# Latent attention on one core: the rope rows' halves exchanged by VectorE, one product tile less, and ScalarE's queue between two pairs of heads in another order

## The chip, the cores and the metric

The kernel runs on one core of a Trainium2 chip. Five engines work side by side and wait for each other by semaphores: TensorE (PE in the rows) multiplies, VectorE (DVE), ScalarE (ACT) and GpSimd (POOL) work element by element, and SyncE (SP) issues loads. The metric is the device time of one execution in microseconds; less is better. Matrix results land in PSUM, eight banks of 128 partitions by 512 fp32 values;

## The reference

The whole kernel computes a two-layer transformer block and then a second two-layer block, for 512 tokens of width 1024, in fp32. The change touches only the last mixer, a latent attention with 16 heads:

```python
q = jnp.einsum('bsr,rhd->bshd', q_c, w_uq)            # q_c: 512 x 256, w_uq: 256 x 16 x (128 + 64)
q_nope, q_rope = q[..., :128], q[..., 128:]
q_rope = apply_rope(q_rope, cos, sin)                 # x1, x2 = halves of 32
k_rope = apply_rope(k_r, cos, sin)
q_lat = jnp.einsum('bshd,rhd->bshr', q_nope, w_uk)
s = q_lat . kv_c + q_rope . k_rope                    # scaled, masked by chunks of 64, softmax in blocks of 128
o = jnp.einsum('bshr,rhd->bshd', p . kv_c, w_uv)
return (o * jax.nn.silu(z)) @ w_out

def apply_rope(x, cos, sin):
    return concatenate([x1 * cos - x2 * sin, x2 * cos + x1 * sin])
```

## The kernel before

Activations are kept transposed: features on the 128 partitions, the 512 tokens along a row. Each fp32 product is made of three matmuls of rounded parts (`mm3`, lines 964 to 966: high by high, high weight by low data, low weight by high data). For that every weight unit, 128 partitions by 1024 columns (eight tiles of 128), goes through four steps: SP loads it into one of four `raw` slots, ScalarE copies it to its high part (`split_hi`, line 540), GpSimd subtracts to get the low part (`split_lo`, line 447), and TensorE uses it. Semaphores count units: `raw_in` loaded, `hi_done`, `w_ready` both parts there, `unit_used` used by TensorE. Unit u needs unit u - 4 used, since the slots are a ring of four.

The order of all work is written out by hand, engine by engine. The latent attention goes over eight pairs of heads. Each pair r takes four units from `u0 = O_H + 2 + 4 r`: two of gate columns z (u0, u0 + 1), one of query weights for the NEXT pair (u0 + 2), and one with the value tiles of this pair and the latent query tiles of the next (u0 + 3). On TensorE a pair runs so (`pair_of_heads`): the first z product; score blocks 0 and 1; four of the eight k-tiles of the second z product; then steps m = 2 to 10, which interleave transposes of the probabilities (`o_transpose`, line 1434), scores (`o_scores`, lines 1423 to 1426) and the product with the latent (`o_latent`, line 1442). Two k-tiles of the second z product stand at m = 5 and two at m = 9. Behind them come `queries` for the next pair, `values` and `latent_queries`. There are eight score blocks m: blocks 0 to 3 are the four query blocks of the first head with 128, 256, 384 and 512 keys, blocks 4 to 7 those of the second.

`queries` makes four tiles: the 128 nope rows of each head into two gate banks, the rope rows of both heads (64 + 64 partitions) into bank 2, and the same rope rows with their halves of 32 exchanged into bank 3. The exchange is in the weights: `pack_weights` lays out tiles `rope` and `swap`.

VectorE's softmax has two steps per block, maximum (`o_max_of`, lines 2083 and 2085) and product with the reciprocal of the sum (`o_norm`, lines 2090 and 2094); ScalarE has the exponential (line 890) between them. At a pair's end VectorE subtracts for the second latent (line 2099), for the two nope tiles (`nope_lo`, line 2067), turns the rope rows (`rotate`, lines 2073 to 2078) and multiplies the two gate products (line 2122). ScalarE at that point applies Silu to z (line 920), makes high parts (lines 902, 869), splits units, copies the latent queries (`keep_latent`, lines 881 and 883), makes the high parts of the rope rows in both partition halves (`rope_hi`, line 876) and scales one eighth of the residual (line 932). GpSimd makes the rope rows' low parts (`rope_lo`, line 507) and multiplies the residual (line 516).

ScalarE's functions come in table sets; a table load (ACT_TABLE_LOAD) is put in by the compiler, once ahead of the first Silu and once ahead of the first Exp of a pair. A loop round holds two pairs, r = 0 and r = 1 (`Fori(0, PAIRS - 2, 2)`), so pairs 0, 2 and 4 stand at the start of a round, and pairs 6 and 7 behind the loop.

Of the kernel before, what the change touches and what calls it, by code (L numbers as in the profile page):

```python
# [37 lines left out]
RING = 4  # L38
# [67 lines left out]
PI = 3.1415925  # L106


def build(nc, xT, weights, cols, rows, c_row, rel, onehot, w2, posc, ada, ws, bs, pcnt, pos, out):

    ctx = ExitStack()
    with ctx:
# [309 lines left out]
        def _(pool):  # L422
# [22 lines left out]
            def split_lo(slot, unit):  # L445
                pool.wait_ge(hi_done, unit + 1)
                pool.tensor_tensor(wsp[:, slot, 1, :], raw[:, slot, :], wsp[:, slot, 0, :].bitcast(F32),  # L447
                                   ALU.subtract).then_inc(w_ready, 1)
# [61 lines left out]
            for u in range(O_C + RING, O_H + 5):  # L510
                split_lo(u % RING, u)
# [6 lines left out]
            with pool.Fori(0, PAIRS - 1) as hp:  # L518
                for k in range(RING):
                    u = O_H + 5 + k  # L520
                    split_lo(u % RING, hp * RING + u)
# [5 lines left out]
            for u in range(O_H + 5 + RING * (PAIRS - 1), UNITS):  # L527
                split_lo(u % RING, u)
# [3 lines left out]
        def _(act):  # L532
            def split_hi(u, i=0):
# [6 lines left out]
                act.activation(wsp[:, u % RING, 0, :], raw[:, u % RING, :], ACT.Copy).then_inc(hi_done, 1)  # L540
# [325 lines left out]
            def nope_hi(r, hp):  # L866
                for e in range(2):
                    act.wait_ge(uq_mm, hp * 3 + (3 * r + e + 1))
                    act.activation(qns[:, e, 0, :], bank[GATE_BANKS[r % 2][e]][:, :], ACT.Copy).then_inc(n_hi, 1)

            def rope_hi(r, hp):

                for e in range(2):
                    act.wait_ge(r_part, hp * 4 + (4 * r + e + 3))
                    for half in range(2):
                        act.activation(qrs[e][0][half * HD:half * HD + HD, :], r_raw[e], ACT.Copy).then_inc(r_hi, 1)
# [27 lines left out]
            def pair_of_heads(r, hp, last):  # L904

                u0 = O_H + 2 + RING * r
                split_hi(u0 + 3, hp)
# [16 lines left out]
                else:  # L924
# [3 lines left out]
                    rope_hi(r + 1, hp)  # L928
                    split_hi(u0 + 6, hp)
                j = hp + r  # L930
                act.wait_ge(mod_x, j + (16 + DC + 1))
                act.activation(hT[:, j, :], hT[:, j, :], ACT.Identity, scale=modg[:, 1, bass.ds(j + 16, 1)],
                               bias=modg[:, 1, bass.ds(j + 24, 1)]).then_inc(alpha_done, 1)

# [9 lines left out]
            rope_hi(0, 0)  # L944
# [16 lines left out]
        def _(pe):  # L961
# [420 lines left out]
            def queries(r, hp, u):  # L1382
# [3 lines left out]
                for n in range(4):  # L1386
                    if first and n == 2:
                        pe.wait_ge(c_normed, 3)
                    if first and n == 3:
                        pe.wait_ge(kr_ready, 1)  # L1390
# [3 lines left out]
                    x.then_inc(uq_mm if n < 3 else unit_used, 1)  # L1394
# [51 lines left out]
            def pair_of_heads(r, hp, last):  # L1446
# [7 lines left out]
                project(u0 + 1, z[1][:, :], hp, part=range(4))  # L1454
                for m in range(2, 11):
                    if m in (5, 9):
                        project(u0 + 1, z[1][:, :], hp, part=range(m // 4 * 2 + 2, m // 4 * 2 + 4))
# [33 lines left out]
        def _(dve):  # L1491
# [780 lines left out]
```

## Times and profile before

| | us |
|---|---|
| three runs | 2046.43, 2047.74, 2047.75 |
| median | 2047.74 |
| the profiled execution | 2044.9 |
| its span | 2043.0 |
| mean granted TensorE clock | 0.988 |
| TensorE busy in the span | 1943.9 (95%) |
| VectorE / ScalarE / GpSimd busy | 972.6 / 836.8 / 815.2 |

The loop over pairs runs from about 1653 to 1924 us of the span. In a row of the timeline the columns are start us, duration us, engine, line, operation, out<-in, shapes, count, and in brackets how long the engine was idle before and what it waited for. A matmul's end is modelled and overlaps the next one's start: TensorE's progress is read from the starts. "x2" or "x4" joins neighbours of one kind, and then the duration is that of all of them.

### The profile page before, as it was taken

How to read it: one execution, taken by the hardware profiler on the slowest of the kernel's cores; microseconds unless marked ns; L12 is line 12 of the kernel's file. 1: busy time of each engine (PE TensorE's matmuls, PEld its weight loads, DVE VectorE, ACT ScalarE, POOL GpSimd, SP SyncE). 2: the span in 40 equal slices, each digit the busy share in tenths (PEclk: the TensorE clock that was granted, in tenths of full speed). 3: DMA queues.
4: the chain of work that ended last, by engine and by line, in shares of the span. 5: the costliest groups of instructions: out<-in, count | busy, mean ns of one | idle time of the engine just before them, and what ended most of it. 6: DMA issues, size and time to landing. Idle time of an engine off the chain costs nothing.

```text
span 2043.0 us, 29277 instructions
## 1 busy us (share of the span) xinstructions
PE 1943.9 (95%) x9688; PEld 1623.0 (79%) x9688; DVE 972.6 (48%) x2289; ACT 836.8 (41%) x1520; POOL 815.2 (40%) x390
## 2 busy tenths in 40 slices
PE   7999999999989999999999998999999799999896
PEld 5897888888777989878888887877888587777784
DVE  5554655321445777456652115557411644545414
ACT  4564222232443777442222224222223356666523
POOL 3633544444374011135454442545444145252440
PEclk9999999999999999999999998999999999999998
DMA  7532554322242122135442222322223122121221
GB/s 242 166 100 95 192 176 169 105 94 92 73 165 75 38 70 78 39 107 194 164 166 100 94 96 77 106 93 98 92 94 102 42 73 73 51 72 52 73 72 41
DMA packets 70027, 209.56 MB, mean 103 GB/s; under 512 B 9739, under 2 KB 15115, under 8 KB 69948
## 3 DMA queue, kind: packets, MB, share of 16 engines
q1 hardware_dynamic: 57724, 174.72, 26.0%
q10 hardware_dynamic: 12224, 33.85, 5.1%
q8 instruction: 42, 0.69, 0.1%
q14 instruction: 37, 0.30, 0.0%
HBM read 196.90 MB, written 8.49 MB: 101 GB/s over the span
## 4 chain that ended last, share of the span: by engine, by line
PE 62%; issue 21%; POOL 9%; DVE 6%; ACT 2%; POOLq 0%; DVEq 0%; ACTq 0%
PE bank L964 16%; PE bank L966 16%; PE bank L965 16%; POOL wsp L447 9%; PE bank L1266 3%; PE bank L1235 1%; PE bank L1246 1%; PE bank L1423 1%; PE bank L1130 1%; PE bank L1442 1%; PE bank L1107 1%; PE bank L1018 1%; PE bank L1434 1%; PE bank L1118 1%; DVE gen L2094 1%
## 5 line engine op out<-in xcount | busy, mean ns | idle before, releaser
L447 POOL TENSOR_TENSOR wsp<-raw,wsp 128x1024 fp32r<-128x1024 f32 x294 | 730.7, 2491 | 1001.9 <-ACT wsp L540 1001.7
L964 PE MATMUL bank<-xs,wsp 128*128 128x512 f32 x1320 | 522.5, 396 | 19.2 <-issue 8.4
L965 PE MATMUL bank<-xs,wsp 128*128 128x512 f32 x1320 | 516.7, 391 | 0.0
L966 PE MATMUL bank<-xs,wsp 128*128 128x512 f32 x1320 | 516.6, 391 | 0.0
L540 ACT ACTIVATE wsp<-raw 128x1024 fp32r<-128x1024 f32 x294 | 307.5, 1052 | 235.3 <-PE bank L966 206.7
L964 PEld LDWEIGHTS bank<-xs,wsp 128*128 128x128 f32 x1320 | 249.6, 189 | 76.1 <-issue 15.1
L964 PE MATMUL bank<-xk,wsp 128*128 128x512 f32 x752 | 293.6, 390 | 9.8 <-DVE xk L1548 5.1
L965 PE MATMUL bank<-xk,wsp 128*128 128x512 f32 x752 | 293.0, 390 | 0.0
L966 PE MATMUL bank<-xk,wsp 128*128 128x512 f32 x752 | 292.9, 390 | 0.0
L966 PEld LDWEIGHTS bank<-xs,wsp 128*128 128x128 f32 x1320 | 249.4, 189 | 52.5
L965 PEld LDWEIGHTS bank<-xs,wsp 128*128 128x128 f32 x1320 | 249.8, 189 | 51.2 <-issue 1.0
L1548 DVE TENSOR_TENSOR xk<-mid,xk 128x512 fp32r<-128x512 f32 x86 | 61.1, 710 | 379.1 <-ACT xk L583 379.1
L583 ACT ACTIVATE xk<-mid 128x512 fp32r (+1 forms) x86 | 54.3, 632 | 324.1 <-PE bank L966 324.1
L964 PEld LDWEIGHTS bank<-xk,wsp 128*128 128x128 f32 x752 | 141.2, 188 | 41.0 <-DVE xk L1548 6.3
L966 PEld LDWEIGHTS bank<-xk,wsp 128*128 128x128 f32 x752 | 141.2, 188 | 29.2
L965 PEld LDWEIGHTS bank<-xk,wsp 128*128 128x128 f32 x752 | 141.3, 188 | 29.1
L1598 DVE CUSTOM_DVE_ANT_0 gen<-gen 128x1024 f32<-128x1024 f32 x48 | 125.8, 2620 | 13.0 <-issue 13.0
L599 ACT ACTIVATE tmp<-tmp 128x512 f32<-128x512 f32 x44 | 27.8, 632 | 245.2 <-DVE tmp L1586 245.2
L1588 DVE TENSOR_TENSOR mid<-bank,rstd 128x512 f32 (+1 forms) x44 | 30.4, 692 | 155.6 <-PE bank L966 155.6
L746 ACT ACTIVATE mid<-mid,stat 128x128 f32<-128x128 f32 (+3 forms) x128 | 70.8, 555 | 35.7 <-DVE stat L1850 35.5
L1266 PE MATMUL bank<-mid 128*128 128x64 f32 x640 | 82.4, 276 | 0.0
L1266 PEld LDWEIGHTS bank<-mid 128*128 128x128 f32 x640 | 77.1, 193 | 0.0
(297 smaller groups left out, 2438.5 us busy)
## 6 DMA issues: line engine op xcount, KB each, us to landing
raw<-weights SPq DMA_DIRECT2D x294, 512.0 KB, 3.5
gen<-ada ACTq DMA_DIRECT2D x48, 512.0 KB, 3.6
tmp<-mid SPq DMA_DIRECT2D x64, 128.0 KB, 3.0
bias_b<-bias_row ACTq DMA_DIRECT2D x1, 4096.0 KB, 37.3
mid<-bias_b SPq DMA_DIRECT2D x8, 512.0 KB, 3.9
hT<-xT SPq DMA_DIRECT2D x2, 1024.0 KB, 9.6
bias_a<-bias_row ACTq DMA_DIRECT2D x1, 2048.0 KB, 17.5
mid<-bias_a SPq DMA_DIRECT2D x8, 256.0 KB, 2.9
```

Of the source, the lines that this page charges most:

```text
L447: pool.tensor_tensor(wsp[:, slot, 1, :], raw[:, slot, :], wsp[:, slot, 0, :].bitcast(F32), ALU.subtract).then_inc(w_ready, 1)
L540: act.activation(wsp[:, u % RING, 0, :], raw[:, u % RING, :], ACT.Copy).then_inc(hi_done, 1)
L583: act.activation(xk[:, k % 2, 0, :], mid[:, i * RING + k, :], ACT.Copy).then_inc(xk_hi, 1)
L599: act.activation(tmp[:, 2 + p, :], tmp[:, p, :], ACT.Silu).then_inc(silu_ready, 1)
L746: act.activation(b_s[b][:, r, 0:w], b_s[b][:, r, 0:w], ACT.Exp, scale=-1.0, bias=stat[:, b, r:r + 1], accum_out=stat[:, b, 4 + r:5 + r]).t ...
L964: pe.matmul(dst, w[0], x[0], start=first, stop=False)
L965: pe.matmul(dst, w[0], x[1], start=False, stop=False)
L966: return pe.matmul(dst, w[1], x[0], start=False, stop=last)
L1266: x = pe.matmul(dst[:, (1 + r) * HD:(2 + r) * HD], b_pt[b][:, r, kb * P:kb * P + P], vtok[:, r, kb * P + pp * HD:kb * P + pp * HD + HD], s ...
L1548: dve.tensor_tensor(xk[:, k % 2, 1, :], mid[:, i * RING + k, :], xk[:, k % 2, 0, :].bitcast(F32), ALU.subtract).then_inc(xk_ready, 1)
L1588: dve.tensor_tensor(mid[:, i * 2 + p, :], bank[2 * p + 1][:, :], rstd[:, :], ALU.mult).then_inc(up_free, 1)
L1598: dve.tensor_tensor_reduce(out=ada_st[k], in0=ada_st[k], in1=cond, scale=1.0, scalar=0.0, op0=ALU.mult, op1=ALU.add, accum_out=mod_sum[:, ...
```

## The change

- `queries` makes three tiles. Bank 3 is no longer written by TensorE there, and `uq_mm` counts two per pair.
- `rotate` goes head by head, with four instructions: 64 rows of bank 2 by cos; two products of 32 rows each by sin, from bank 2 into the other half's rows of bank 3; and the difference. The first head's rotation stands where `rotate` stood, the second's behind the two gate products. `r_part` counts six per pair.
- ScalarE: `rope_hi` is called per head. The split of u0 + 3, which opened a pair, is now at the end of the pair before, between the two heads; behind the residual stands an Exp of one column, then the second head's copies.
- TensorE: 3 + 2 + 3 k-tiles of the second z product, where there were 4 + 2 + 2.
- The splits of the query unit take 768 columns and those of the value unit 512 (`columns_of`); the loads stay at 1024. The weights' layout is as it was.

```diff
+def columns_of(u):
+    return (768, 512, UNIT, UNIT)[(u - O_H) % 4] if O_H <= u < O_O else UNIT
...
             for u in range(O_C + RING, O_H + 5):
-                split_lo(u % RING, u)
+                split_lo(u % RING, u, columns_of(u))
...
-            def rope_hi(r, hp):
-
-                for e in range(2):
-                    act.wait_ge(r_part, hp * 4 + (4 * r + e + 3))
-                    for half in range(2):
-                        act.activation(qrs[e][0][half * HD:half * HD + HD, :], r_raw[e], ACT.Copy).then_inc(r_hi, 1)
+            def rope_hi(e, r, hp):
+
+                act.wait_ge(r_part, hp * 6 + (6 * r + 3 * e + 3))
+                for half in range(2):
+                    act.activation(qrs[e][0][half * HD:half * HD + HD, :], r_raw[e], ACT.Copy).then_inc(r_hi, 1)
...
                 u0 = O_H + 2 + RING * r
-                split_hi(u0 + 3, hp)
                 for m in range(10):
...
                     keep_latent(r + 1, hp)
-                    rope_hi(r + 1, hp)
+                    rope_hi(0, r + 1, hp)
                     split_hi(u0 + 6, hp)
+                    split_hi(u0 + 7, hp)
...
                                bias=modg[:, 1, bass.ds(j + 24, 1)]).then_inc(alpha_done, 1)
+                if not last:
+                    act.activation(credit[:, 10:11], eps[:, 0:1], ACT.Exp)
+                    rope_hi(1, r + 1, hp)
...
-            rope_hi(0, 0)
+            rope_hi(0, 0, 0)
+            rope_hi(1, 0, 0)
+            split_hi(O_H + 5)
...
-                for n in range(4):
+                for n in range(3):
                     if first and n == 2:
                         pe.wait_ge(c_normed, 3)
-                    if first and n == 3:
-                        pe.wait_ge(kr_ready, 1)
...
-                    x.then_inc(uq_mm if n < 3 else unit_used, 1)
+                    x.then_inc(uq_mm if n < 2 else unit_used, 1)
...
-                project(u0 + 1, z[1][:, :], hp, part=range(4))
+                project(u0 + 1, z[1][:, :], hp, part=range(3))
                 for m in range(2, 11):
                     if m in (5, 9):
-                        project(u0 + 1, z[1][:, :], hp, part=range(m // 4 * 2 + 2, m // 4 * 2 + 4))
+                        project(u0 + 1, z[1][:, :], hp, part=range(3, 5) if m == 5 else range(5, DC))
...
-            def rotate(r, hp):
-
-                dve.wait_ge(unit_used, hp * RING + (O_H + 1 + RING * r))
-                dve.tensor_tensor(tmp[:, 0, :], bank[2][:, :], cosb, ALU.mult).then_inc(r_part, 1)
-                dve.tensor_tensor(bank[3][:, :], bank[3][:, :], sinb, ALU.mult).then_inc(r_part, 1)
-                dve.wait_ge(r_part, hp * 4 + (4 * r + 2))
-                for e in range(2):
-                    half = slice(e * HD, e * HD + HD)
-                    dve.tensor_tensor(r_raw[e], tmp[half, 0, :], bank[3][half, :], ALU.add).then_inc(r_part, 1)
+            def rotate(e, r, hp):
+
+                head = slice(e * HD, e * HD + HD)
+                if e == 0:
+                    dve.wait_ge(unit_used, hp * RING + (O_H + 1 + RING * r))
+                dve.tensor_tensor(tmp[head, 0, :], bank[2][head, :], cosb[head, :], ALU.mult).then_inc(r_part, 1)
+                for src, dst in ((0, 32), (32, 0)):
+                    at = slice(e * HD + src, e * HD + src + 32)
+                    x = dve.tensor_tensor(bank[3][e * HD + dst:e * HD + dst + 32, :], bank[2][at, :], sinb[at, :], ALU.mult)
+                x.then_inc(r_part, 1)
+                dve.wait_ge(r_part, hp * 6 + (6 * r + 3 * e + 2))
+                dve.tensor_tensor(r_raw[e], tmp[head, 0, :], bank[3][head, :], ALU.subtract).then_inc(r_part, 1)
...
-                    rotate(r + 1, hp)
+                    rotate(0, r + 1, hp)
...
+                if not last:
+                    rotate(1, r + 1, hp)
```

Three places in the order of instructions. The first is ScalarE between pair 6 and pair 7, from the first split behind `nope_hi` on. Before (L540 is a split, L881 and L883 `keep_latent`, L876 `rope_hi`, L932 the residual, L890 the exponential):

```order
L540 ACTIVATE wsp<-raw 128x1024 [waits unit_used,raw_in0]
L881 ACTIVATE gen<-bank4 128x512 [waits lat_mm]
L883 ACTIVATE gen<-bank5 128x512 [waits unit_used]
L876 ACTIVATE mid_r<-tmp 64x512 [waits r_part]
L876 ACTIVATE mid_r<-tmp 64x512
L876 ACTIVATE mid_r<-tmp 64x512 [waits r_part]
L876 ACTIVATE mid_r<-tmp 64x512
L540 ACTIVATE wsp<-raw 128x1024 [waits unit_used,raw_in1]
L932 ACTIVATE hT<-hT,modg 128x512 [waits mod_x]
L540 ACTIVATE wsp<-raw 128x1024 [waits unit_used,raw_in2]
L890 ACT_TABLE_LOAD
L890 ACTIVATE bank0,stat<-bank0,stat 128x128 [waits o_nm]
```

In the changed kernel (L546, L886, L888, L881, L937 and L895 are the same things, L940 the new Exp):

```order
L886 ACTIVATE gen<-bank4 128x512 [waits lat_mm]
L888 ACTIVATE gen<-bank5 128x512 [waits unit_used]
L881 ACTIVATE mid_r<-tmp 64x512 [waits r_part]
L881 ACTIVATE mid_r<-tmp 64x512
L546 ACTIVATE wsp<-raw 128x768 [waits unit_used,raw_in1]
L546 ACTIVATE wsp<-raw 128x1024 [waits unit_used,raw_in2]
L937 ACTIVATE hT<-hT,modg 128x512 [waits mod_x]
L940 ACT_TABLE_LOAD
L940 ACTIVATE credit<-eps 128x1
L881 ACTIVATE mid_r<-tmp 64x512 [waits r_part]
L881 ACTIVATE mid_r<-tmp 64x512
L895 ACTIVATE bank0,stat<-bank0,stat 128x128 [waits o_nm]
```

The split that stood between the residual and the first exponential is now ahead of the residual, and the table load and the new Exp stand ahead of the second head's two copies. (This split has 1024 columns only here, in front of pair 7; elsewhere it has 512.)

The second place is ScalarE at the start of a loop round. Before:

```order
L945 ISA
L539 ISA [waits raw_in2]
L540 ACT_TABLE_LOAD
L540 ACTIVATE wsp<-raw 128x1024 [waits unit_used]
L889 ISA
L890 ACTIVATE bank6,stat<-bank6,stat 128x128 [waits o_nm]
```

In the changed kernel, the end of a round, and behind the dots its start:

```order
L937 ACTIVATE hT<-hT,modg 128x512
L940 ACT_TABLE_LOAD
L940 ACTIVATE credit<-eps 128x1
L879 REGISTER_ALU
L881 ACTIVATE mid_r<-tmp 64x512 [waits r_part]
L881 ACTIVATE mid_r<-tmp 64x512
L955 REGISTER_ALU
L955 COMPARE_AND_BRANCH
...
L955 ISA
L895 ACT_TABLE_LOAD
L895 ACTIVATE bank6,stat<-bank6,stat 128x128 [waits o_nm]
```

A table load stands at a round's start in both. The one ahead of the new Exp, at the round's end, comes to it.

The third is VectorE at the end of a pair, here pair 6. Before (L2067 is `nope_lo`, L2073 to L2078 `rotate`, L2122 the gate products, L2083 the next pair's first maximum):

```order
L2067 TENSOR_TENSOR gsp<-bank6,gsp 128x512 [waits n_hi]
L2067 TENSOR_TENSOR gsp<-bank7,gsp 128x512 [waits n_hi]
L2073 TENSOR_TENSOR tmp<-bank2,gen 128x512 [waits unit_used]
L2074 TENSOR_TENSOR bank3<-bank3,gen 128x512
L2078 TENSOR_TENSOR tmp<-tmp,bank3 64x512 [waits r_part]
L2078 TENSOR_TENSOR tmp<-tmp,bank3 64x512
L2122 TENSOR_TENSOR mid<-bank0,mid 128x512 [waits z_ready,uv_mm]
L2122 TENSOR_TENSOR mid<-bank1,mid 128x512 [waits z_ready,uv_mm]
L2083 TENSOR_REDUCE stat<-bank0 128x1 [waits o_qk]
```

In the changed kernel (L2075, L2083 to L2089, L2133 and L2094):

```order
L2075 TENSOR_TENSOR gsp<-bank6,gsp 128x512 [waits n_hi]
L2075 TENSOR_TENSOR gsp<-bank7,gsp 128x512 [waits n_hi]
L2083 TENSOR_TENSOR tmp<-bank2,gen 64x512 [waits unit_used]
L2086 TENSOR_TENSOR bank3<-bank2,gen 32x512 x2
L2089 TENSOR_TENSOR tmp<-tmp,bank3 64x512 [waits r_part]
L2133 TENSOR_TENSOR mid<-bank0,mid 128x512 [waits z_ready,uv_mm]
L2133 TENSOR_TENSOR mid<-bank1,mid 128x512 [waits z_ready,uv_mm]
L2083 TENSOR_TENSOR tmp<-bank2,gen 64x512
L2086 TENSOR_TENSOR bank3<-bank2,gen 32x512 x2
L2089 TENSOR_TENSOR tmp<-tmp,bank3 64x512 [waits r_part]
L2094 TENSOR_REDUCE stat<-bank0 128x1 [waits o_qk]
```

The four instructions between `nope_lo` and the gate products (two over all 128 partitions, two over 64) have become four for the first head alone; the same four for the second head stand behind the gate products, ahead of the maximum.

## Rows read from the trace of the kernel before

**Rows 1.** The profile page's first line.
```profile
span 2043.0 us, 29277 instructions
```
**Rows 2.** Table of stages, one pair of heads.
```profile
1728.90:1763.30 34.40, 33.34 (x179) 27.32 (x177) 16.99 (x43) 21.73 (x45) 13.19 (x8) 1.00 0.18 61
```
**Rows 3.** Timeline of TensorE, end of a pair.
```profile
1748.88 0.48 PE L964 MATMUL bank<-gsp,wsp 128*128 128x512 f32 x1
...
1752.83 0.39 PE L966 MATMUL bank<-gsp,wsp 128*128 128x512 f32 x1
...
1754.42 0.39 PE L964 MATMUL bank<-xk,wsp 128*128 128x512 f32 x1
...
1757.14 0.39 PE L964 MATMUL bank<-xs,wsp 128*128 128x512 f32 x1
```
**Rows 4.** Timeline of VectorE, the same stretch.
```profile
1752.53 0.69 DVE L2067 TENSOR_TENSOR gsp<-bank,gsp 128x512 fp32r<-128x512 f32 x1 [0.40 <-ACT gsp L869]
1754.62 0.69 DVE L2073 TENSOR_TENSOR tmp<-bank,gen 128x512 f32<-128x512 f32 x1 [1.40 <-PE bank L966]
...
1763.17 0.29 DVE L2083 TENSOR_REDUCE stat<-bank 128x1 f32<-128x128 f32 x1 [4.50 <-PE bank L1426]
```
**Rows 5.** Timeline of ScalarE, from this pair into the next.
```profile
1757.34 0.60 ACT L883 ACTIVATE gen<-bank 128x512 f32<-128x512 f32 x1
1757.84 2.59 ACT L876 ACTIVATE mid_r<-tmp 64x512 fp32r<-64x512 f32 x4
...
1761.41 0.80 ACT L932 ACTIVATE hT<-hT,modg  x1
1762.12 1.04 ACT L540 ACTIVATE wsp<-raw 128x1024 fp32r<-128x1024 f32 x1
1763.18 1.28 ACT L890 ACT_TABLE_LOAD   x1
1764.47 0.34 ACT L890 ACTIVATE bank<-bank,stat 128x128 f32<-128x128 f32 x1
```
**Rows 6.** Timeline of TensorE, the next pair.
```profile
1762.58 0.38 PE L1423 MATMUL bank<-gen 128*128 128x128 f32 x2
...
1766.45 0.27 PE L1434 MATMUL bank<-ident,gen 128*128 128x128 f32 x1
1766.55 0.81 PE L1423 MATMUL bank<-gen 128*128 128x384 f32 x2
...
1767.55 0.38 PE L1434 MATMUL bank<-ident,gen 128*128 128x128 f32 x2
...
1770.11 0.55 PE L1434 MATMUL bank<-ident,gen 128*128 128x128 f32 x3 [0.63 <-DVE gen L2094]
...
1780.29 0.39 PE L966 MATMUL bank<-xs,wsp 128*128 128x512 f32 x1
1781.04 0.66 PE L1434 MATMUL bank<-ident,gen 128*128 128x128 f32 x4 [0.36 <-DVE gen L2094]
```
**Rows 7.** Timeline of VectorE, the first two products.
```profile
1765.16 0.35 DVE L2094 TENSOR_SCALAR gen<-bank,stat 128x128 f32<-128x128 f32 x1
...
1766.86 0.48 DVE L2094 TENSOR_SCALAR gen<-bank,stat 128x256 f32<-128x256 f32 x1
```
**Rows 8.** Groups by line and shape: the nearest rows for new operations.
```profile
L2058 DVE TENSOR_TENSOR bank<-bank,gen 64x512 f32<-64x512 f32 x1 | 0.7, 700 | 0.0
...
L554 ACT ACTIVATE credit<-eps 128x1 f32<-128x1 f32 x1 | 0.2, 203 | 0.0
```
**Rows 9.** Timeline of GpSimd, rope_lo of two heads.
```profile
1759.18 2.61 POOL L507 TENSOR_TENSOR mid_r<-tmp,mid_r 64x512 fp32r<-64x512 f32 x2 [3.27 <-ACT mid_r L876]
```
**Rows 10.** Timelines of VectorE and TensorE before the first pair.
```profile
1650.39 1.29 DVE L2067 TENSOR_TENSOR gsp<-bank,gsp 128x512 fp32r<-128x512 f32 x2
...
1651.95 0.48 PE L964 MATMUL bank<-gsp,wsp 128*128 128x512 f32 x1
```
**Rows 11.** Waits from 1650 to 1895: total us, times, longest.
```profile
PE bank L1434 <- DVE gen L2094: 7.0, 14, 0.7
```

More of the change, by code:

```diff
@@ L442, in _, with split_lo @@
             pool.memset(credit[:, 8:9], 0.0).then_inc(za_silu, 2)
-            def split_lo(slot, unit):
+            def split_lo(slot, unit, w=UNIT):
                 pool.wait_ge(hi_done, unit + 1)
-                pool.tensor_tensor(wsp[:, slot, 1, :], raw[:, slot, :], wsp[:, slot, 0, :].bitcast(F32),
+                pool.tensor_tensor(wsp[:, slot, 1, 0:w], raw[:, slot, 0:w], wsp[:, slot, 0, 0:w].bitcast(F32),
                                    ALU.subtract).then_inc(w_ready, 1)
@@ L520, in _ @@
                     u = O_H + 5 + k
-                    split_lo(u % RING, hp * RING + u)
+                    split_lo(u % RING, hp * RING + u, columns_of(u))
                     if k == 0:
@@ L527, in _ @@
             for u in range(O_H + 5 + RING * (PAIRS - 1), UNITS):
-                split_lo(u % RING, u)
+                split_lo(u % RING, u, columns_of(u))
         @block.scalar
@@ L539, in split_hi @@
                     act.wait_ge(unit_used, i * RING + (u + 1 - RING))
-                act.activation(wsp[:, u % RING, 0, :], raw[:, u % RING, :], ACT.Copy).then_inc(hi_done, 1)
+                w = columns_of(u + i * RING if isinstance(i, int) else u)
+                act.activation(wsp[:, u % RING, 0, 0:w], raw[:, u % RING, 0:w], ACT.Copy).then_inc(hi_done, 1)
             def scaled_hi(gain, base):
@@ L867, in nope_hi @@
                 for e in range(2):
-                    act.wait_ge(uq_mm, hp * 3 + (3 * r + e + 1))
+                    act.wait_ge(uq_mm, hp * 2 + (2 * r + e + 1))
                     act.activation(qns[:, e, 0, :], bank[GATE_BANKS[r % 2][e]][:, :], ACT.Copy).then_inc(n_hi, 1)
-            def rope_hi(r, hp):
-                for e in range(2):
-                    act.wait_ge(r_part, hp * 4 + (4 * r + e + 3))
-                    for half in range(2):
-                        act.activation(qrs[e][0][half * HD:half * HD + HD, :], r_raw[e], ACT.Copy).then_inc(r_hi, 1)
+            def rope_hi(e, r, hp):
+                act.wait_ge(r_part, hp * 6 + (6 * r + 3 * e + 3))
+                for half in range(2):
+                    act.activation(qrs[e][0][half * HD:half * HD + HD, :], r_raw[e], ACT.Copy).then_inc(r_hi, 1)
             def keep_latent(r, hp):
@@ L2123, in pair_of_heads @@
                                       ).then_inc(mid_ready, 1)
+                if not last:
+                    rotate(1, r + 1, hp)
             nope_lo(0, 0)
-            rotate(0, 0)
+            rotate(0, 0, 0)
+            rotate(1, 0, 0)
             with dve.Fori(0, PAIRS - 2, 2) as hp:
```

## The prediction

> **What bounds the kernel now.** I read the page's span first, then the table of stages. The edit touches only the attention loop, where one pair of heads takes 34.4 us and TensorE is busy for 33.3 us of it at a granted clock of 1.00 (2.4 GHz) [rows 1, 2]. So a matmul that is taken out should shorten the span unless something else is then late. TensorE's own timeline gives the price of a matmul: the rows print about 390 ns each, but they overlap, and what counts is from start to start. From 1748.88 to 1752.83 there are 17 starts in 3.95 us; over whole stretches, 12 matmuls (values and latent queries) lie between 1754.42 and 1757.14: 2.72/12 = 0.227 us each [rows 3].
>
> Next I looked for the gaps inside one pair. There are two, both while TensorE waits for the normalised probabilities: before the three transposes of 1770.11, and before the four of 1781.04 [rows 6]. The table of waits has 14 of this kind over the seven pairs [rows 11]. The second gap runs from the end of the last z matmul's turn (1780.29 + 0.23 = 1780.52) to 1781.04: 0.52 us. Everything else I count from s, the start of a pair's first score matmul, which is 1762.58 here.
>
> **Part 1, no product tile.** `queries` loses two mm3 groups, six matmuls: 6 x 0.227 = 1.36 us. It runs once ahead of the loop and at seven boundaries between pairs. Is it on the path there? What follows it waits for other engines. The values wait for the low half of the second latent and the latent queries for the second `nope_lo`, which starts on VectorE at 1752.53 and lasts 0.69, so ends at 1753.22 [rows 4]. The values will start at 1754.42 - 1.36 = 1753.06 (VectorE's subtraction for them is before that `nope_lo` in its queue) and the latent queries, 6 matmuls later, at 1754.42. Room: 1.2 us. The whole 1.36 counts, and the next pair's scores start at 1762.58 - 1.36 = 1761.22. Seven boundaries: 9.5 us.
>
> At the first `queries` it is different. There `nope_lo` ends at 1650.39 + 1.29 = 1651.68, held by the keys' rotation, which does not move; the latent queries started at 1651.95 [rows 10]. They can come at about 1651.8: 0.2 us gained, the rest becomes a new wait.
>
> **Part 2, the rotation in halves.** Four VectorE instructions become eight. The 64x512 product from PSUM, crossing partitions, lasted 0.70 us [rows 8]; a 32x512 one is not in the trace. Free size and not partitions set these times (128x512 0.69, 64x512 0.70 [rows 4, 8]), so I take 0.70; the bounds are the small VectorE rows at 0.35 [rows 7] and twice the nearest, 1.4. `rotate(0)`: starts when bank 2 is complete, 1.36 us sooner than 1754.62, at 1753.26; four steps of 0.7 end at 1756.1. The two gate products (1.29) follow, to 1757.4, and `rotate(1)` ends at 1760.2. Behind it in VectorE's queue is the first maximum, which can start 0.59 after s, at 1761.81 [rows 4, 7]: 1.6 us of room, so these 2.8 us of extra VectorE work cost nothing. Without that cover each would count in full.
>
> **Part 3, ScalarE's order.** I lay the new queue out with the times of the old one [rows 5]. The second latent copy, at 1757.34, comes at 1755.98; 0.50 later, at 1756.48, the first head's two copies (2.59/4 = 0.65 each), to 1757.8; by then `rotate(0)` is done. A split costs 1.05 for 1024 columns; 0.83 for 768 and 0.6 for 512 scale from that with the 0.63 of the 512-column copy as a check; with the overlap of 0.09 that successive rows show they end at 1759.1. The residual (0.80) ends at 1759.9, the table load 1.28 and the dummy Exp 0.20 [rows 8] at 1761.3, the second head's copies at 1762.6. So the first exponential starts at s + 1.4. It was at 1764.47, s + 1.89, behind a 1024-column split and the load. The load has moved from in front of the exponential to a place where ScalarE had time, and `split_hi(u0 + 7)` with it.
>
> The POOL queue: `rope_lo` for the second head now waits for copies that end at 1762.6 and lasts 1.3 [rows 9], to 1763.9. It is first wanted by the fifth score block, after 1770.11. The splits behind it are 768 and 512 wide and wanted a pair later. For the first head it ends near 1759.1, 2 us ahead of the scores. No cost. SP's loads follow these splits, and are hidden as before.
>
> **Part 4, three z matmuls moved.** Between the first two score blocks and the first transpose stand 9 matmuls and no longer 12, and at the end of the pair 9 and no longer 6. The first transpose is asked for at s + 1.11 + 9 x 0.227 = s + 3.2. Its data came 1.04 after the exponential (1764.47 to 1765.16 + 0.35), now s + 2.4. Scores of block 2 start at s + 3.3 and end at s + 4.3; the second transposes need the second product, which ended at 1766.86 + 0.48 = 1767.34, 2.87 after the first exponential, so s + 4.3 [rows 5 to 7]. That just fits. Then the chain maximum, exponential, product of block 2 is 0.68 earlier and the wait of 1770.11 stays as long as it was. At the end of the pair the three extra matmuls (0.68) fill the 0.52 gap and run 0.16 beyond. Net: 0.52 us in each of eight pairs, 4.2 us.
>
> **Part 5, loop heads.** The order listing shows two loads of the table at the start of a loop round: the dummy's, and one still in front of the first exponential of r = 0. This concerns pairs 2 and 4; pair 0 has only the second, pair 6 stands behind the loop and has only the first. In those two the first exponential starts at s + 1.4 + 1.28 = s + 2.7. The second product ends at s + 5.6, the second transposes wait for it, and block 2's product follows at s + 7.9 and not s + 6.85: 1.05 us each, 2.1 us lost. Pair 7's split between the two rope copies is 1024 wide and not 512: 0.45 us later on ScalarE, 0.4 lost.
>
> Where a page and the rows differ: the load's row lasts 1.28 us, the split in front ends at 1762.12 + 1.04 = 1763.16, the load starts at 1763.18 and the exponential at 1764.47 [rows 5], so nothing else is paid around it. The Trainium skill ("ScalarE: Activation LUTs", section "What ACT_TABLE_LOAD costs") gives the same 1283 ns and adds a drain of about 1380 ns for a switch of sets, 2.66 us in all; by that rule the result is the third case below, and the trace does not agree with it.
>
> **Sum.** 9.5 + 0.2 + 4.2 - 2.1 - 0.4 = 11.4 us. The profiled execution took 2044.9 us (span 2043.0 [rows 1] and 1.9 around it), so 2033.5. The median of the runs shown is 2047.74, 2.8 above it; the same gain gives 2036.3.
>
> **The rivals.**
> Second case, ScalarE late at every boundary: the margin of Part 4 (second product at s + 4.3 against 4.3) is nothing. If ScalarE's new queue is 0.6 us longer than my sum of rows (six hand-overs at 0.1 more each), five boundaries lose 0.6 and two more lose it on top of theirs: 4.2 us. Gain 7.2, time 2040.5. For it: nine instructions in a row on one engine. Against: the old queue's rows follow each other within 0.02 to 0.1 us. The other way, if the second load costs nothing, the gain is 13.5: 2034.2.
> Third case, no measurable difference: a table load holds ScalarE for twice its row, 2.6 us. Then the first exponential comes at s + 2.7 in the five boundaries with one load, which by Part 5 costs 1.05 us each, and another 2.6 later in the two with two loads, where the wait is already on the path: 5.3 + 5.2 = 10.5 us. Gain 1.3, time 2046.4. For it: the load is moved in front of other work of this engine, where no row shows one. Against it: the rows of Part 5, with nothing around the load.
> Fourth case, slower: the 32-row products. `rotate(1)` ends after four of them and holds the maximum and, through the second head's copies, the first exponential. Each extra e on one costs 4e - 1.1 a boundary (1.1 is the room between 1760.2 and the copies' start at 1761.3). To eat the 11.4 us and 4.1 more takes 2.2 us at each of seven, e = 0.83: a 32x512 product of 1.53 us. It decides from there; at 1.7 us (e = 1.0, 2.9 us a boundary) the kernel is at 2056.6. Nothing but the missing row speaks for it; the 64-row one at 0.70 speaks against.
> That the change does less than it says is in Part 5: two of seven loads are doubled, not moved.
>
> **Chances.** Forecast case 0.64, the second with its faster wing 0.24 (0.18 and 0.06), the third 0.08, the fourth 0.04. A difference under 0.2% (4.1 us) is what a measurement here cannot tell from none. Faster than that: the first two, 0.88; within: 0.08; slower: 0.04. The range holds the first two cases: 2032.8 to 2041.5.
>
> **What would show it.** TensorE's starts from the first query matmul to the first z matmul 6.9 us apart, not 8.26; a pair of 32.5 us, and 33.6 where the loop starts a round; no gap before the four last transposes; the 32x512 rows at 0.70; the load before the second head's copies, and the first exponential at s + 1.4. Wrong if the second transposes wait at every pair, or if a new gap stands before the latent queries inside the loop.

## The result, and the profile after

| | before | changed |
|---|---|---|
| median of four runs, us | 2047.09 | 2033.74 |
| lowest and highest | 2045.34, 2047.75 | 2032.06, 2035.49 |
| span of the profiled execution | 2043.0 | 2030.2 |
| ratio, 95% interval | | 0.9936 [0.9922, 0.9949] |

The forecast was 2036.3 (2032.8 to 2041.5). The kernel is 13.4 us faster by the medians and 12.8 by the spans, where the sum said 11.4. (The forecast started from a median before of 2047.74; the fourth run put it at 2047.09, and that is 0.65 of the 2.6 us between 2036.3 and 2033.74.) In the changed kernel line numbers are 5 to 14 higher; L974 to L976 are the three matmuls of `mm3`, L1431 to L1434 the scores, L1442 the transposes, L1450 the product with the latent.

The table of stages, cut at the first score matmul of pairs 1, 3 and 4, answers to [rows 2]. Its first column is the stretch, its second the length; the busy times of PE, PE's weight loads, DVE, ACT and POOL follow, and the granted clock is the third column from the right:

```profile
1691.56:1724.11 32.55, 31.84 (x171) 26.27 (x170) 19.84 (x46) 21.20 (x45) 11.54 (x7) 1.00 0.20 65
1757.71:1790.28 32.57, 31.86 (x171) 26.26 (x170) 19.84 (x46) 21.20 (x45) 11.56 (x7) 1.00 0.20 64
1790.28:1823.88 33.60, 32.30 (x171) 26.18 (x170) 19.75 (x46) 22.52 (x46) 11.52 (x7) 1.00 0.19 62
```

A pair takes 32.55 us where it took 34.5, and 33.6 at the start of a loop round. VectorE is busy 2.8 us more in a pair than before. ScalarE is busy 1.3 us more in the last row than in the two above it: that is the second table load.

TensorE through pair 3, which starts at s = 1757.71, answers to [rows 6] and, in the last two lines, to [rows 3]:

```profile
1757.71 0.38 PE L1431 MATMUL bank<-gen 128*128 128x128 f32 x2
...
1760.89 0.27 PE L1442 MATMUL bank<-ident,gen 128*128 128x128 f32 x1
1761.00 0.81 PE L1431 MATMUL bank<-gen 128*128 128x384 f32 x2
...
1762.00 0.38 PE L1442 MATMUL bank<-ident,gen 128*128 128x128 f32 x2
...
1764.56 0.55 PE L1442 MATMUL bank<-ident,gen 128*128 128x128 f32 x3 [0.64 <-DVE gen L2105]
...
1775.65 0.60 PE L1442 MATMUL bank<-ident,gen 128*128 128x128 f32 x4
...
1777.91 0.47 PE L974 MATMUL bank<-gsp,wsp 128*128 128x512 f32 x1
...
1782.12 0.39 PE L974 MATMUL bank<-xk,wsp 128*128 128x512 f32 x1
```

The first transpose is at s + 3.18 (before 3.87), the third step at s + 6.85 with its wait unchanged at 0.64, and the last four transposes at s + 17.94 (before 18.46) have no bracket any more: their gap is filled. From the queries' start to the values are 4.21 us; before it was 5.54. To the first z matmul, which follows the latent queries at 1784.84, it is 6.93, where the prediction said 6.9.

ScalarE ahead of pair 3 answers to [rows 5]:

```profile
1752.46 0.60 ACT L888 ACTIVATE gen<-bank 128x512 f32<-128x512 f32 x1
1752.96 1.28 ACT L881 ACTIVATE mid_r<-tmp 64x512 fp32r<-64x512 f32 x2
1754.26 1.37 ACT L546 ACTIVATE wsp<-raw 128x768 fp32r<-128x768 f32 x2
1755.53 0.80 ACT L937 ACTIVATE hT<-hT,modg  x1
1756.35 1.28 ACT L940 ACT_TABLE_LOAD   x1
1757.64 0.20 ACT L940 ACTIVATE credit<-eps 128x1 f32<-128x1 f32 x1
1757.75 1.27 ACT L881 ACTIVATE mid_r<-tmp 64x512 fp32r<-64x512 f32 x2
1758.93 0.31 ACT L895 ACTIVATE bank<-bank,stat 128x128 f32<-128x128 f32 x1
```

From the first head's copies at 1752.96 to the second head's, nine instructions follow each other without a gap, and the first exponential starts at s + 1.22 (before 1.89, forecast 1.4; the rows behind the load overlap by 0.09 each). The load is 1.28 us long, and the gaps around it are 0.02 and 0.01. Ahead of pair 2, at the start of a round (s = 1724.11), the same engine shows both loads:

```profile
1722.76 1.28 ACT L940 ACT_TABLE_LOAD   x1
...
1725.45 1.28 ACT L895 ACT_TABLE_LOAD   x1
1726.74 0.34 ACT L895 ACTIVATE bank<-bank,stat 128x128 f32<-128x128 f32 x1
```

The exponential is at s + 2.63 there. The 32-row products, by line and shape, answer to [rows 8]: 0.70 us, as the 64-row one.

```profile
L2086 DVE TENSOR_TENSOR bank<-bank,gen 32x512 f32<-32x512 f32 x32 | 22.4, 700 | 0.7
```

Executions of one and the same program differ by up to 6 us (the changed kernel in the last experiment: 2033.88 to 2040.08). The experiments are therefore compared by a stretch that holds little of that noise: from the first query matmul to the first value matmul of the last pair, called D below. It is 278.10 us before and 265.91 in the changed kernel, 12.19 less. Each D comes from one profile; the changed kernel's second profile gave 265.76, so a difference of 0.2 in D alone says nothing. A number like s + 6.86 is that of an ordinary pair.

| kernel | exp. 0 | 2nd transposes | 3rd step | last transposes | pair | pair at a round's start | D |
|---|---|---|---|---|---|---|---|
| before | 1.89 | 4.97 | 7.53 | 18.45 | 34.48 | 34.46 | 278.10 |
| changed | 1.22 | 4.30 | 6.86 | 17.94 | 32.55 | 33.60 | 265.91 |
| z cut 4 + 2 + 2 again | 1.22 | 4.97 | 7.53 | 18.44 | 33.12 | 33.47 | 268.91 |
| swap tile again | 1.44 | 4.43 | 6.85 | 17.94 | 33.91 | 35.13 | 276.27 |
| tile and quarters only | 2.51 | 5.44 | 7.65 | 18.56 | 33.23 | 33.23 | 269.41 |
| the same, z 3 + 2 + 3 | 2.51 | 5.44 | 7.65 | 18.73 | 33.34 | 33.35 | 269.63 |
| no extra Exp | 1.61 | 4.64 | 6.86 | 17.94 | 32.54 | 32.54 | 263.77 |
| ScalarE's loop written out | 1.22 | 4.30 | 6.86 | 17.93 | 32.54 | 32.53 | 263.64 |
| wide splits | 1.86 | 4.86 | 7.06 | 18.14 | 32.75 | 34.21 | 268.57 |
| quarters doubled | 3.00 | 6.00 | 8.21 | 19.31 | 33.91 | 36.28 | 282.04 |
| z 2 + 1 + 2 + 3, written out | 1.22 | 4.31 | 6.43 | 17.51 | 32.13 | 32.12 | 260.55 |
| z 2 + 1 + 2 + 3, no extra Exp | 1.60 | 4.66 | 6.84 | 17.92 | 32.53 | 32.56 | 263.76 |

(The pair at a round's start is the mean of pairs 2 and 4.)

### The profile page after: what moved, and what is told of

It reads as the page before. It is cut to its first block, busy times and chain, and to the rows that moved or that the text cites. A ratio compares the mean times of both kernels' runs of the same rounds, so it can differ in the third digit from the quotient of the medians.

```text
span 2030.2 us, 29228 instructions
## 1 busy us (share of the span) xinstructions
PE 1931.9 (95%) x9640; PEld 1612.8 (79%) x9640; DVE 995.0 (49%) x2321; ACT 834.2 (41%) x1529; POOL 801.1 (39%) x390
## 4 chain that ended last, share of the span: by engine, by line
PE 61%; issue 21%; POOL 9%; DVE 6%; ACT 2%; POOLq 0%; DVEq 0%; ACTq 0%
PE bank L974 15%; PE bank L976 15%; PE bank L975 15%; POOL wsp L452 9%; PE bank L1276 3%; PE bank L1245 1%; PE bank L1450 1%; PE bank L1256 1%; PE bank L1140 1%; PE bank L1431 1%; PE bank L1442 1%; PE bank L1117 1%; PE bank L1028 1%; PE bank L1128 1%; PE bank L1272 1%
## 5 line engine op out<-in xcount | busy, mean ns | idle before, releaser
L452 POOL TENSOR_TENSOR wsp<-raw,wsp 128x1024 fp32r<-128x1024 f32 (+2 forms) x294 | 716.8, 2443 | 985.9 <-ACT wsp L546 985.8
L974 PE MATMUL bank<-xs,wsp 128*128 128x512 f32 x1320 | 521.6, 395 | 19.1 <-issue 8.4
L976 PE MATMUL bank<-xs,wsp 128*128 128x512 f32 x1320 | 516.0, 391 | 0.0
L546 ACT ACTIVATE wsp<-raw 128x1024 fp32r<-128x1024 f32 (+2 forms) x294 | 301.4, 1034 | 235.1 <-PE bank L976 206.1
L974 PEld LDWEIGHTS bank<-xs,wsp 128*128 128x128 f32 x1320 | 249.4, 189 | 75.9 <-issue 14.7
L974 PE MATMUL bank<-xk,wsp 128*128 128x512 f32 x752 | 293.6, 390 | 9.7 <-DVE xk L1556 5.1
L976 PE MATMUL bank<-xk,wsp 128*128 128x512 f32 x752 | 293.0, 390 | 0.0
L976 PEld LDWEIGHTS bank<-xs,wsp 128*128 128x128 f32 x1320 | 248.9, 189 | 52.4
L974 PEld LDWEIGHTS bank<-xk,wsp 128*128 128x128 f32 x752 | 141.3, 188 | 41.2 <-DVE xk L1556 6.3
L976 PEld LDWEIGHTS bank<-xk,wsp 128*128 128x128 f32 x752 | 141.4, 188 | 29.5
```

The lines of the kernel that those rows point to most:

```text
L452: pool.tensor_tensor(wsp[:, slot, 1, 0:w], raw[:, slot, 0:w], wsp[:, slot, 0, 0:w].bitcast(F32), ALU.subtract).then_inc(w_ready, 1)
L546: act.activation(wsp[:, u % RING, 0, 0:w], raw[:, u % RING, 0:w], ACT.Copy).then_inc(hi_done, 1)
L974: pe.matmul(dst, w[0], x[0], start=first, stop=False)
L976: return pe.matmul(dst, w[1], x[0], start=False, stop=last)
```

## The experiments

**The z tiles moved back.**

```diff
-                project(u0 + 1, z[1][:, :], hp, part=range(3))
+                project(u0 + 1, z[1][:, :], hp, part=range(4))
...
-range(3, 5) if m == 5 else range(5, DC)
+range(4, 6) if m == 5 else range(6, DC)
```

> The changed kernel with the second z product cut 4 + 2 + 2 again (s is the start of a pair's first score matmul). Theory A, everything behind s is the later of two chains: in ordinary pairs the third transpose step goes back from s + 6.86 to s + 7.53, the last transposes from s + 17.94 to s + 18.45 with their gap of 0.35 to 0.5 us in front; in the two pairs with two table loads (third step already at s + 7.87) the last transposes come 0.17 earlier. Sum about +2.5 us, span 2032.7. Rival B: the move is worth the same 0.5 us in all eight pairs: +4.2, span 2034.4. Rival C: the move is worth nothing beside the removed tile: span 2030.2.

Measured: 2038.81 us, ratio 0.9962 [0.9948, 0.9976]; D 3.00 above the changed kernel's, 2.5 expected. An ordinary pair loses 0.57, but a pair at a round's start gains 0.13 (33.60 to 33.47): its third step is held by the late exponential in either cut (7.86), and only the overrun at the end goes. The move is not worth the same in all pairs; rivals B and C fall. The sum missed 0.06 a pair: from the last transposes to the next s it is 14.68 here and 14.62 in the changed kernel, where these transposes do not wait.

**The swap tile computed again.**

```diff
-    return (768, 512, UNIT, UNIT)[(u - O_H) % 4] if O_H <= u < O_O else UNIT
+    return (UNIT, 512, UNIT, UNIT)[(u - O_H) % 4] if O_H <= u < O_O else UNIT
...
-                for n in range(3):
+                for n in range(4):
...
-                    x.then_inc(uq_mm if n < 2 else unit_used, 1)
+                    if n != 2:
+                        x.then_inc(uq_mm if n < 2 else unit_used, 1)
```

> The changed kernel, but the six matmuls of the exchanged rope rows are done again (into bank 3, where VectorE overwrites them; the query unit's splits are 1024 wide for it). Theory A: each boundary between pairs +1.37 us, the start +0.3, two pairs with two table loads +0.2 from the wider split: +10.2 us, span 2040.4. Rival B: the tile was partly hidden, and the gain came from the new order: below +6 us, span under 2036.

Measured: 2045.57 us, ratio 0.9998 [0.9989, 1.0008]; D 10.36 above the changed kernel's, 10.2 expected. Ordinary pairs lose 1.36; those at a round's start lose 1.53, of which the wider split is 0.2. The six matmuls count in full, rival B falls, and they are the largest part of the change: with them back, the median cannot be told from the one before, and D is 1.83 below it.

**Only the tile and the rotation.** ScalarE's and VectorE's order as before the change, z cut 4 + 2 + 2:

```diff
                 u0 = O_H + 2 + RING * r
+                split_hi(u0 + 3, hp)
...
                     rope_hi(0, r + 1, hp)
+                    rope_hi(1, r + 1, hp)
                     split_hi(u0 + 6, hp)
-                    split_hi(u0 + 7, hp)
...
-                if not last:
-                    act.activation(credit[:, 10:11], eps[:, 0:1], ACT.Exp)
-                    rope_hi(1, r + 1, hp)
...
                     rotate(0, r + 1, hp)
+                    rotate(1, r + 1, hp)
...
-                if not last:
-                    rotate(1, r + 1, hp)
```

> Only the removed tile and the rotation in quarters (and narrower splits): both rotations ahead of the gate products, the old order on ScalarE without the extra Exp, z cut 4 + 2 + 2. Theory A: first exponential at s + 2.35, second transposes at about s + 5.3, third step at s + 7.5 as in the kernel before; each pair 33.06 us, the two gaps of a pair as before; about 9.7 us gained on the kernel before, span 2033.3. Rival B: without the new order on ScalarE the extra VectorE work (2.8 us a pair) lies on the path: gain below 5 us, span over 2038.

Measured: 2036.13 us, ratio 0.9953 [0.9936, 0.9969]; D 8.69 below the kernel before, 9.7 expected. So this part alone brings seven tenths of the gain, and rival B falls. The missing 1.0 is in the third step: s + 7.65, not 7.5, in pairs 1 to 5 and s + 8.18 in pair 7, since the first exponential is at s + 2.51, not 2.35. ScalarE waits for the second head's rotation, and the exponential is 0.16 later than I summed. The next kernel has the same order on ScalarE; its timeline ahead of pair 1 (s = 1693.65) shows the wait of 1.28 us and the load that ends against the exponential:

```profile
1691.46 1.29 ACT L881 ACTIVATE mid_r<-tmp 64x512 fp32r<-64x512 f32 x2 [1.28 <-DVE tmp L2086]
1692.78 0.85 ACT L546 ACTIVATE wsp<-raw 128x768 fp32r<-128x768 f32 x1
...
1694.87 1.28 ACT L895 ACT_TABLE_LOAD   x1
1696.16 0.34 ACT L895 ACTIVATE bank<-bank,stat 128x128 f32<-128x128 f32 x1
```

**The same with z cut 3 + 2 + 3.** As the kernel above, and:

```diff
-                project(u0 + 1, z[1][:, :], hp, part=range(4))
+                project(u0 + 1, z[1][:, :], hp, part=range(3))
```

> As the kernel with only the removed tile and the rotation in quarters, but z cut 3 + 2 + 3. Theory A: the tile move pays only with the first exponential early. Here it stays at s + 2.35, the third transpose step at s + 7.55, and the extra matmuls at the end run 0.17 beyond the gap: last transposes at s + 18.65, 1.4 us over eight pairs slower than that kernel, span 2034.7. Rival B: the move fills the 0.5 us gap whatever ScalarE does: 4 us faster than that kernel, span 2029.

Measured: 2038.08 us, ratio 0.9955 [0.9938, 0.9971]; D 0.22 above the kernel before it in this list. Theory A had the mechanism but 1.4 us was too much: pairs 1 to 6 are 0.11 longer each (0.17 expected), and pair 0, whose exponential is early in this order (s + 1.74), gains 0.55. Rival B's 4 us are not there: without an early exponential the tile move buys nothing. ScalarE's new order on its own brings little, 0.50 of D (269.41 here above, 268.91 with the z tiles moved back); it is what lets the tile move pay.

**No extra Exp.**

```diff
                 if not last:
-                    act.activation(credit[:, 10:11], eps[:, 0:1], ACT.Exp)
                     rope_hi(1, r + 1, hp)
```

> The changed kernel without the one-column Exp. Theory A: one table load a pair, in front of the first exponential; the second head's copies start when the second rotation is done (0.3 later than ScalarE is free), so the first exponential comes at s + 1.6 in every pair; second transposes at s + 4.6, third step still at s + 6.86. The two pairs with two loads gain 1.0 us each: span 2028.2, faster than the changed kernel. Rival B: the early load is what makes room; five pairs lose 0.3 us and two gain 1.0: span 2029.7. Rival C: without it the exponential is as late as before the change: slower, span above 2032.

Measured: 2030.07 us, ratio 0.9924 [0.991, 0.9937]; D 2.14 below the changed kernel's. ScalarE ahead of pair 3 (s = 1757.82):

```profile
1756.83 1.29 ACT L881 ACTIVATE mid_r<-tmp 64x512 fp32r<-64x512 f32 x2 [0.38 <-DVE tmp L2088]
1758.13 1.28 ACT L895 ACT_TABLE_LOAD   x1
1759.43 0.34 ACT L895 ACTIVATE bank<-bank,stat 128x128 f32<-128x128 f32 x1
```

The exponential is at s + 1.61 in each pair but the first (1.87), 0.39 later than with the extra Exp in ordinary pairs, and the third step stays at s + 6.86; rivals B and C fall. The line of code that moves the load brings nothing and costs 2.1 us through the second load at two rounds' starts.

**ScalarE's loop written out.**

```diff
+            split_hi(O_H + 5)
+            act.activation(credit[:, 10:11], eps[:, 0:1], ACT.Exp)
             rope_hi(1, 0, 0)
-            split_hi(O_H + 5)
-            with act.Fori(0, PAIRS - 2, 2) as hp:
+            for hp in range(0, PAIRS - 2, 2):
```

> The changed kernel with ScalarE's loop over pairs written out (so no load is put in at a round's start), and the extra Exp also ahead of the second head's copies for pair 0. Theory A: the third transpose step of pairs 2 and 4 goes from s + 7.87 to s + 6.86, of pair 0 from s + 7.05 to 6.86: 2.2 us, span 2028.0. Rival B: the second load was hidden or the longer instruction stream costs as much: span 2030.

Measured: 2030.66 us, ratio 0.9932 [0.9919, 0.9946]; D 2.27 below the changed kernel's, 2.2 expected. The same end by another way: one load ahead of a pair's exponentials, and here the first exponential is at s + 1.22 in pairs 1 to 6 (s + 1.11 in pair 0, 1.65 in pair 7 with its wide split).

**Wide splits.** `columns_of` returns UNIT for all units.

> The changed kernel with all splits 1024 wide. Theory A: ScalarE's queue at a boundary is 0.2 + 0.43 us longer, the first exponential at s + 1.85; the third step is at the later of s + 6.86 and 2.21 behind the second transposes: +0.2 in four pairs and pair 7, +0.6 in pairs 0, 2 and 4: about +2.8 us, span 2033.0. Rival B: the narrower splits are covered and bring nothing: span 2030.2.

Measured: 2038.27 us, ratio 0.9966 [0.9954, 0.9978]; D 2.66 above the changed kernel's, 2.8 expected. Exponentials at s + 1.87 and 3.27, third steps at 7.07 and 8.50: theory A by place and size. The narrower copies are worth a fifth of the gain, although ScalarE is busy for 21.2 of an ordinary pair's 32.55 us and GpSimd for 11.5.

**Quarters doubled.** Each 32-row product once more, into a row of `tmp` that nothing reads:

```diff
+                for src, dst in ((0, 32), (32, 0)):
+                    more = slice(e * HD + src, e * HD + src + 32)
+                    dve.tensor_tensor(tmp[e * HD + dst:e * HD + dst + 32, 1, :], bank[2][more, :], sinb[more, :], ALU.mult)
                 for src, dst in ((0, 32), (32, 0)):
```

> The changed kernel with each 32-row product done once more into an unused row (four extra instructions of 0.7 us a pair). Theory A: the second rotation ends 2.8 us later, at about s + 1.8, the copies behind it push the first exponential to s + 3.1 (with two loads s + 4.4), the third transpose step to about s + 8.25 and s + 9.55; pair 0 loses 2.7: +13 us, span 2043, about the kernel before. Rival B: VectorE's time is covered: below +3 us. Rival C: it counts in full, 2.8 us in each of eight pairs: +22 us, span 2052.

Measured: 2050.45 us, ratio 1.0025 [1.0015, 1.0034]; D 16.13 above the changed kernel's, 13 expected. Ordinary pairs do what theory A says (exponential s + 3.00, third step s + 8.21). The 3 us above it are in pairs 0, 2 and 4, where the exponential comes last of all (s + 4.66, 4.41 and 4.41). Rivals B and C fall. TensorE in pair 0 (s = 1659.33), and the stages around it:

```profile
1665.09 0.33 PE L1442 MATMUL bank<-ident,gen 128*128 128x128 f32 x1 [2.44 <-DVE gen L2108]
...
1667.28 1.92 PE L1431 MATMUL bank<-gen 128*128 128x512 f32 x2
1668.21 1.42 PE L1433 MATMUL bank<-gen_r,mid_r 128*128 128x512 f32 x1
```

```profile
1659.00:1664.00 5.00, 3.65 (x20) 2.79 (x18) 2.10 (x5) 3.18 (x5) 1.96 (x3) 1.00 0.00 0
1664.00:1666.50 2.50, 1.32 (x5) 0.74 (x5) 1.28 (x6) 2.13 (x6) 2.50 (x3) 1.00 0.29 67
1666.50:1669.00 2.50, 2.08 (x5) 1.05 (x6) 1.69 (x5) 0.95 (x3) 1.63 (x1) 0.62 0.37 146
```

Behind the wait of 2.44 us, and one of 0.52 at the second transposes, the granted clock falls: 1.00 up to 1666.50, and 0.62 on average over the next stretch, so it is at the lower of its two levels for a part of it; the 512-key scores last 1.92 and not 1.02 us. The third step is 3.35 behind the second transposes there (2.59 and 3.32 in pairs 2 and 4), and 2.21 in the ordinary pairs.

**One more z tile moved, between block 2 and the second transposes**, on the kernel with the written-out loop:

```diff
-                project(u0 + 1, z[1][:, :], hp, part=range(3))
+                project(u0 + 1, z[1][:, :], hp, part=range(2))
                 for m in range(2, 11):
+                    if m == 3:
+                        project(u0 + 1, z[1][:, :], hp, part=range(2, 3))
```

> The changed kernel with ScalarE's loop written out, the extra Exp also for pair 0, and z cut 2 + 1 + 2 + 3: two k-tiles behind the first two score blocks, one between score block 2 and the second transposes. Theory A: the third transpose step is 2.21 behind the second, which needs the second product (2.94 behind the first exponential) and no longer the matmuls in front: s + 6.5 where it was s + 6.86, in pairs 0 to 6; pair 7 has a wide split ahead of its exponential and gains nothing. 2.5 us less than the written-out kernel between the first query matmul and the last pair's values: 261.1 where that had 263.64. Rival B: the first transposes now wait and give it back: 263.6 or more.

Measured: 2028.67 us, ratio 0.9913 [0.99, 0.9927]; D 260.55, 3.09 below the written-out loop's, 2.5 expected. TensorE in pair 3 (s = 1756.35), and VectorE's product for block 1 with the maximum of block 2 behind it:

```profile
1758.85 0.27 PE L1443 MATMUL bank<-ident,gen 128*128 128x128 f32 x1
...
1760.65 0.39 PE L1443 MATMUL bank<-ident,gen 128*128 128x128 f32 x2
...
1762.78 0.55 PE L1443 MATMUL bank<-ident,gen 128*128 128x128 f32 x3 [0.20 <-DVE gen L2108]
```

```profile
1760.03 0.48 DVE L2108 TENSOR_SCALAR gen<-bank,stat 128x256 f32<-128x256 f32 x1
1760.43 0.55 DVE L2097 TENSOR_REDUCE stat<-bank 128x1 f32<-128x384 f32 x1
```

Neither of the first two steps waits, and the wait at the third falls from 0.64 to 0.20; rival B falls. The third step is at s + 6.43 and not 6.5: it is not tied to the second transposes but to the second product, which ends at 1760.51, 2.27 ahead of it. This is the best version found.

**The same cut without the extra Exp**, the loop as in the changed kernel.

> The changed kernel without the extra Exp, z cut 2 + 1 + 2 + 3. Theory A: the first exponential is at s + 1.6, so the second transposes stay at s + 4.64 whatever TensorE does in front, and the third step at s + 6.85: nothing gained on the kernel without the Exp; 263.8 us from the first query matmul to the last values, as that had. Rival B: the gain comes from the order of matmuls alone: 261.3.

Measured: 2031.81 us, ratio 0.9929 [0.9915, 0.9942]; D 263.76, as without the third cut (263.77). The same order of matmuls, with an exponential 0.38 later, gains nothing. So the early exponential has a use, only not in the kernel that it was put in.

**The changed kernel again, beside these two.**

> The changed kernel as it is, timed beside the two others on the same chip: between the first query matmul and the last pair's values 265.9 us as in its first profile; median about 3 to 5 us above the kernel with z cut 2 + 1 + 2 + 3 and the written-out loop if theory A holds, equal to it if not.

Measured: 2035.60 us, ratio 0.995 [0.9937, 0.9964], 6.9 us above the best version; the two intervals do not meet. D is 265.76. By D the best version is 5.2 us ahead, where the expectations for the two said 4.8; the rest of the 6.9 lies outside the stretch or in the spread of the runs (last section).

## Why the prediction was right

By its own steps, on D, where the sum's five terms lie:

- **Queries at seven boundaries: 9.5 forecast, 9.84 measured** (from the last transposes of a pair to the next s, 14.62 where it was 16.02). The matmul price of 0.227 from start to start was right; the printed duration of 0.39 would have given 16. The experiment with the swap tile confirms it from the other side: 1.36 a boundary, 9.5 in seven. The 0.3 above the forecast belong to the moved z tiles, behind which the last transposes no longer wait: with the tiles moved back this stretch is 14.68.
- **The start: 0.2 forecast, 0.45 measured.** The new wait is there, with `nope_lo` as its end, but the latent queries start at 1651.95 as before and not at 1651.8; as D's stretch begins 0.11 later, that is 0.1 of the forecast 0.2. The rest was not forecast: TensorE entered its loop without the pause that it had before (0.43 from the last latent query at 1653.19 to the first z matmul; now 0.22), and from there to s it took 5.44 us where it had taken 5.55.

```profile
1651.95 0.47 PE L974 MATMUL bank<-gsp,wsp 128*128 128x512 f32 x1 [1.00 <-DVE gsp L2075]
```

- **The z tile move, the second load and pair 7: 4.2 - 2.1 - 0.4 = 1.7 forecast, 1.88 measured** between s and the last transposes. Pairs 1, 3, 5 and 6 gain 0.50 to 0.54 (0.52 forecast); pairs 2 and 4 lose 0.51 and 0.53 (0.53 forecast, from s + 2.7 and s + 7.9; measured 2.63 and 7.87). Two pairs missed in opposite directions. Pair 0 gains 0.30: the step "pair 0 has only the second" took the one load for harmless. But ahead of pair 0 the second head's copies wait 1.62 us for their rotation, and both a split and the load stand behind them, so that the exponential is at s + 1.90 (s = 1658.83; before s + 1.11):

```profile
1657.48 1.29 ACT L881 ACTIVATE mid_r<-tmp 64x512 fp32r<-64x512 f32 x2 [1.62 <-DVE tmp L2089]
1658.79 0.63 ACT L546 ACTIVATE wsp<-raw 128x512 fp32r<-128x512 f32 x1
1659.44 1.28 ACT L895 ACT_TABLE_LOAD   x1
1660.74 0.34 ACT L895 ACTIVATE bank<-bank,stat 128x128 f32<-128x128 f32 x1
```

The written-out loop has the split and the load ahead of these copies, and its pair 0 has the exponential at s + 1.11. Pair 7 gains 0.55 and not 0.1: "0.45 us later on ScalarE, 0.4 lost" took the margin for nothing, but second transposes 0.34 later still leave the third step to TensorE (4.64 + 2.21 = 6.85; measured 6.94, as in pair 6). That the sum of this line comes within 0.2 is partly luck: pair 0 gave 0.2 less than forecast and pair 7 0.4 more.
- **The margin that "just fits"** does fit: the second product ends at s + 4.16 and the second transposes start at s + 4.30 without a wait. In the pairs of all kernels the third step starts at the later of two times: 3.56 behind the scores of block 2 (1761.00 to 1764.56; before 1766.55 to 1770.11), or 2.27 behind the end of the second product. Where the second transposes wait for that product, the latter is 2.21 behind their start. In pairs 6 and 7 both are 0.09 longer, and why was not looked into. With z cut 3 + 2 + 3 the third step is at s + 6.86 as long as the second transposes come by s + 4.65, 0.35 later than they do.
- **VectorE's eight instructions cost nothing at the seven boundaries**: 0.70 us each as taken, and the second rotation (its last row: `1755.99 0.69 DVE L2089`) ends at 1756.68, 1.0 before ScalarE takes it up at 1757.75. Ahead of pair 0 ScalarE does wait for it, as shown above. The fourth rival's rule was tested by doubling: it said 4 x 0.7 - 1.1 = 1.7 us an ordinary boundary, the pairs lengthened by 1.36. Its price was a little high, since part of the delay goes into the margin of 0.35.
- The second case (ScalarE later by hand-overs) is refuted by the row of nine instructions without a gap, the third (a load that costs twice its row) by the exponential that starts 0.01 behind the load. The drain of about 1380 ns that the Trainium skill adds to a load ("ScalarE: Activation LUTs", section "What ACT_TABLE_LOAD costs") does not show in the rows of any kernel here: every load in this loop lasts 1.28 us, with 0.02 ahead of it and 0.01 behind. (The third case's own sum is off by 0.4: 11.4 - 10.5 leaves a gain of 0.9 and not 1.3.)

In total 12.19, where 11.4 were forecast; so the mechanism was as forecast, and the misses are small terms. The span fell by 12.8: 0.1 us came ahead of the stretch as a loss, and 0.7 behind it as a gain, which no part of the change touches.

## What to carry to other kernels

Price a matmul from start to start, and take a wait apart into the two chains that meet in it. Here one rule with two constants (3.56 behind the scores of block 2, 2.27 behind the end of the product of block 1, each 0.09 more in the last two pairs) accounts for the pairs of all these kernels, but for three in which the clock fell. An earlier start is worth nothing until the engine that it feeds can use it: the exponential 0.4 us earlier brought nothing in the changed kernel, and with one more z tile moved it brought 3 us. Look in the order of instructions for loads that a compiler puts in at a loop's head: here an instruction that loads a table in the last line of a loop body saved nothing for the next round, since the load at the loop's head came all the same.

## What the runs showed that was not expected

The same program twice, the tail behind the last value matmuls (L974 on xk), first the changed kernel, then its repetition:

```profile
1912.10:1932.10 20.00, 18.50 (x75) 14.78 (x76) 4.08 (x6) 6.13 (x9) 9.54 (x4) 0.91 0.22 80
...
2004.10:2030.20 26.10, 9.79 (x25) 4.20 (x24) 16.31 (x22) 11.31 (x17) 0.00 (x0) 0.83 0.22 81
```

```profile
1912.60:1932.60 20.00, 18.49 (x70) 14.63 (x71) 4.08 (x6) 6.14 (x9) 8.61 (x4) 0.83 0.24 80
...
2004.60:2033.70 29.10, 12.77 (x31) 5.88 (x29) 17.56 (x24) 11.38 (x17) 0.00 (x0) 0.81 0.20 73
```

From the last values to the end it took 118.05 and 121.04 us. In both, TensorE has just waited 2.50 and 1.45 us; the granted clock is 0.91 in the one and 0.83 in the other, and starts of matmuls are 0.43 us apart while it is at the lower level. Of the 3.0 us, 1.3 have arisen by the matmul at 2007.40 (2009.18 in the repetition); the other 1.7 are in the next group of 16 matmuls, which takes 7.10 us in the one and 8.80 in the other. Over all kernels this tail is 117.0 to 121.1 us, and the first query matmul lies between 1646.1 and 1648.7, though no edit touches either. So where TensorE waits, the clock that follows differs between executions of one program, and kernels that are 1 to 3 us apart are told from each other more surely by a stretch without such waits than by a few runs. What decides in an execution whether the clock falls was not found.
